# Four modulation units of layer 1 computed during layer 0's top-k rounds, the last two weight steps of three products taken together per token tile, and four row products moved to GpSimd

## Chip, cores, metric

The kernel runs on one core of a Trainium2 chip. The metric is the device time of one launch in microseconds, median of three runs. Everything is float32; products that need full precision are split into a high and a low half in the rounded format `float32r` and done as three matmuls.

## What is computed

A two-layer diffusion-style transformer block (512 image tokens, 256 context tokens, width 1024) followed by a second, causal block. Cut to what matters:

```python
for i in range(2):                                   # "layer 0" and "layer 1"
    mods  = silu(c)     @ ada_w[i] + ada_b[i]        # 6 x 1024 modulation values from a vector
    cmods = silu(c_ctx) @ ada_w[i] + ada_b[i]
    h  = rms_norm(x, n1) * (1 + sc1) + sh1           # same for the context rows
    p  = h @ w_in[i]                                 # five conv columns, window attention, global attention
    x  = x + g1 * (concat(ya, yb, yc, yd) @ w_out[i])            # "mix"
    h2 = rms_norm(x, n2) * (1 + sc2) + sh2
    aff = softmax(h2 @ router)                       # 16 experts
    gates, idx = top_k(aff.T, capacity)              # 64 image tokens, 32 context tokens per expert
    y  = (silu(xs @ w_gate) * (xs @ w_up)) @ w_down  # per expert, on the tokens picked
    x  = x + g2 * scatter_add(y * gates)
x = rms_norm(x, final_g)                             # then the second block:
x = x + concat(gated_deltanet(..), dilated_attention(..)) @ w_out_2      # on rms_norm(x, ln1_2)
x = x + (silu(conv(h @ w_gate_2)) * (h @ w_up_2)) @ w_down_2             # h = rms_norm(x, ln2_2)
out = rms_norm(x, ln_f_2)
```

Context rows are needed in layer 0 only. `ada_w[i]` is 1024 x 6144; a **modulation unit** `(l, u)` is the product with 512 of its columns, so there are 12 units a layer.

## The kernel before

It is written per engine: functions `sync`, `tensor`, `scalar`, `vector` and `gpsimd` each issue one engine's instructions in a fixed order, with semaphore waits that name what they need (`P[...]` from TensorE, `A[...]` ScalarE, `V[...]` VectorE, `G[...]` GpSimd). Tables shared by all five set the order of mixed work: `attention_plan` and `experts_plan`.

**Weights.** `weight_steps` lists every weight load, 1 MB each, in the order of use. SyncE issues them one after the other (L723). Each goes into a slot: three slots of `RING`, a fourth that is the context half of `X` (layer 1 and later), three of `WIDE`. `WIDE` shares its memory with `WHL`, which holds split weights; so a `WIDE` load waits until the last product with split weights (`ld["after"]`) is over. A load waits also until the step that last used its slot is over, and whatever stands behind it in SyncE's list waits too. The row stores of layer 0 (`xrows` L701: the tokens, to which the experts' results are added by scatter; `hrows` L704: the normalised tokens, from which later experts gather) stand in the same list, ahead of the load marked `rows`.

**Modulation units** (`ada`): two loads, for each 4 x 32-column matmuls into one bank (L772), ScalarE copies the row to `ROW4` (L1319), TensorE turns it (L764), VectorE adds the bias (L1826). Units 0 to 3 of layer 0 are done at the start. The other 8 of layer 0 and all 12 of layer 1 are spread over layer 0's attention, one for each pair of heads in `attention_plan`; a pair is scores (L901, L898), softmax on VectorE and ScalarE (L2078, L1445), two flips (L910, copied by L1458), values (L921, L926) and background work such as `spread` (L857).

**Mix**: `tokens` does a product of token tiles (6 in layer 0, 4 later) with a weight of 8 x 128 rows, half of the columns at a time, in four steps of 256 rows. A step does six matmuls on each tile in turn (L1090 to L1092). The results are read tile by tile after the last step of a half: VectorE scales (L2126) and GpSimd or VectorE adds to `X` (L2594, L2129); in the second half `behind` runs the norm as well, ScalarE squares (L1322), takes the root (L1326) and VectorE scales the tile (L1845). In this order VectorE takes tile t's sum, then tile t-1's mean square, then tile t-2's scaling, and after the last tile all that is left.

**Route**: TensorE turns the tiles (L782, L756), ScalarE and VectorE copy them (L1484, L2138), router product (L951), softmax, then eight rounds of top-8 on VectorE (L2171, L2173), a scan for the places (L2177, L2179), and `posT` on TensorE (L971), after which the experts' tokens are selected (L2207) and picked (L1037, L1040).

**Experts**: 12 loads each; per load 4 matmuls with the image tokens (L983), 4 with the context tokens in layer 0 (L989).

**Between the blocks**: for each of four tiles, `final_g` multiplies the tile (L2506, VectorE), ScalarE squares the tile and the product (L1322), roots, and VectorE scales the product (L2500); both norms are made from these. At its end the second block has two products in the form of `tokens`, `mix2` and `down2`, each followed by a norm through `behind`.

Of the kernel before, what the change touches and what calls it, by code (L numbers as in the profile page):

```python
# [8 lines left out]
ALU = mybir.AluOpType  # L9
# [6 lines left out]
LOOK = 2  # L16

# [79 lines left out]
def weight_steps(ada_w, w_in, w_out, w_gate, w_up, w_down, w_in2, w_out2, w_gate2, w_up2, w_down2):  # L97
# [29 lines left out]
    for l in range(2):  # L127
# [5 lines left out]
        if l == 0:  # L133
            ada(0, range(4, 12))
            ada(1, range(12))
        for half in (0, 512):
            add(w_out[l, :, half:half + 512], 8, 512, "k")
        for e in range(17):
# [7 lines left out]
            if e == 0:  # L146
                wide = len(loads) - 4
# [5 lines left out]
        for ld in loads[wide - 4:]:  # L153
            ld["expert"] = True
    for c0 in (0, 512, 1024):
        add(w_in2[:, c0:c0 + 512], 8, 512, "f")
# [18 lines left out]

    turn, slots, last, count = -1, (), {}, {}
    q, last_q, nq, wide, split = -1, {}, 0, None, None
    for ld in loads:
        turn, slots = (0 if ld["slots"] != slots and slots[:3] != ld["slots"][:3] else turn + 1), ld["slots"]
        k = slots[turn % len(slots)]  # L180
# [15 lines left out]
    for used in range(len(steps)):  # L196
# [4 lines left out]
        while done < len(steps) and done <= used + LOOK:  # L201
            if used < mix <= done:
                break
# [8 lines left out]
def attention_plan(l, need_ctx):  # L212
# [5 lines left out]
    units = [(0, u) for u in range(4, 12)] + [(1, u) for u in range(12)] if need_ctx else []  # L218
# [290 lines left out]
def program(nc, vecs, rows, frow, heads, consts, hconst, bias, x, ctxt, ada_w, w_in, w_out, router,  # L509
            w_gate, w_up, w_down, w_in2, w_out2, w_gate2, w_up2, w_down2, out):  # L510
    with ExitStack() as es:
# [103 lines left out]
        ONES = TM1[0:48, :]  # L615
# [40 lines left out]
        XG, HN2, JUNK = ar(0, 4, 1024), ar(4096, 4, 1024), [ar(8192, 1024), ar(9216, 1024)]  # L656
# [73 lines left out]
        def tensor(e):  # L730
# [351 lines left out]
            def tokens(ring, name, on, k, n, hi, lo_, nt=4):  # L1082
                st, h, lo = weights()
                for t in range(nt):
# [3 lines left out]
                    for i in range(2):  # L1088
                        j = n + i
                        e.matmul(o, hi(j)[:, z], h[:, i, :], start=j == 0, stop=False)  # L1090
                        e.matmul(o, hi(j)[:, z], lo[:, i, :], start=False, stop=False)  # L1091
                        ins = e.matmul(o, lo_(j)[:, z], h[:, i, :], start=False, stop=j == k - 1)  # L1092
                    names = [(*name, t)] if n == k - 2 else []
                    if t == nt - 1:
                        ins.then_inc(pe, P(("w", st["i"]), *names))
                    elif names:
                        ins.then_inc(pe, P(*names))
# [180 lines left out]
            for half in range(2):  # L1278
                for n in range(0, 8, 2):
                    tokens(every, ("mix2", half), V, 8, n, lambda j: YH2[j], lambda j: YL2[j])  # L1280
            turn_tiles(HN3, "2c", lambda j: ("x3T", j), lambda j: (V, ("x3T", j)))
            for part, r0, pairs in ffn_plan():
                columns([(V, ("gate", f)) for f, _ in pairs], "x3T")
                columns([(V, ("gu", f)) for f, _ in pairs])
                if pairs[-1][0] == FFN[part][1] // 128 - 1:
                    nf = (FFN[part][1] - r0) // 128
                    e.wait_ge(dve, V["gl", FFN[part][1] // 128 - 1])
                    for half in range(2):
                        for n in range(0, nf, 2):
                            tokens(every, ("down2", part, half), V, nf, n, lambda j: GH[:, j, :], lambda j: GL[:, j, :])  # L1290


        def scalar(e):
# [185 lines left out]
            def route(l, need_ctx):  # L1479
# [11 lines left out]
                e.activation(aff, aff, ACT.Exp).then_inc(act, A(("eaff", l)))  # L1491

# [284 lines left out]
            for half in range(2):  # L1777
                tokens(8)
            normalise(HN3, "2c", [(dve, V["mix2", 1, t]) for t in range(4)])
# [996 lines left out]
```

## Time and profile before

| | |
|---|---|
| median of 3 runs | 2863.82 us (2863.59 to 2863.98) |
| profiled execution, device time | 2861.94 us |
| its span, first to last instruction | 2860.1 us |
| TensorE matmuls busy | 2589.9 us, 91% |
| VectorE, ScalarE, GpSimd busy | 46%, 35%, 12% |
| mean granted TensorE clock | 0.963 |
| moved from and to DRAM | 567.72 MB, mean 198 GB/s |

Where the time lies, by the span's own clock: start and layer 0's first product to 200 us, layer 0 attention to 387, mix to 455, route to 508, experts to 1112, layer 1 attention to 1379, mix to 1425, route to 1470, experts to 1989, the turn to the second block to 2030, the second block to 2860. A busy share of 91% says that most of the span is TensorE's, but not in which stage something else ends last; this is read from the timelines of the stages. A row of a timeline gives start, duration, engine, line, the operation, and in brackets the idle time before it with the engine that ended it.

### The profile page before, as it was taken

To read this page: it belongs to the slowest core of one execution; us is meant where nothing else is said; L and a number is where in the kernel's file an instruction comes from. 1 tells how busy PE (TensorE), PEld (TensorE's weight loads), DVE (VectorE), ACT (ScalarE), POOL (GpSimd) and SP (SyncE) were. 2 spreads that over 40 slices of the span, in tenths; PEclk is the share of its full clock that TensorE was granted. 3 is DMA by queue.
4 is the path that set the end of the run, shared out by engine and by line. 5 is a ranking of instruction groups with operands and counts; after the bars stand their busy time and mean duration, and the time that the engine had idled before them with its cause. 6 is when DMAs were issued, how large, how long until landed. Compare 5 with 4: busy or idle time off the path is not lost.

```text
span 2860.1 us, 35448 instructions
## 1 busy us (share of the span) xinstructions
PE 2589.9 (91%) x13952; PEld 1523.0 (53%) x13952; DVE 1312.8 (46%) x2567; ACT 1004.2 (35%) x1857; POOL 348.5 (12%) x186
## 2 busy tenths in 40 slices
PE   6999996999999996987869999997899997999998
PEld 3875575322222222764733333332567786787886
DVE  2597545344444444676342333323654654443342
ACT  4226542343444444446322222221343333322222
POOL 0210020010011101210200000000114220222221
PEclk9999998999999998999979999999899898999999
DMA  7218732799999998210139999999120002223221
GB/s 249 74 45 281 250 103 103 267 320 367 366 362 366 361 371 270 85 60 1 64 143 386 386 386 386 386 386 349 31 89 30 16 12 79 95 89 98 94 81 52
DMA packets 303036, 567.72 MB, mean 198 GB/s; under 512 B 12624, under 2 KB 55760, under 8 KB 302744
## 3 DMA queue, kind: packets, MB, share of 16 engines
q1 hardware_dynamic: 294480, 545.33, 53.5%
q0 software_dynamic: 3616, 11.80, 1.8%
q10 hardware_dynamic: 4776, 8.33, 0.9%
q8 instruction: 112, 1.84, 0.3%
q14 instruction: 52, 0.43, 0.0%
HBM read 550.74 MB, written 14.68 MB: 198 GB/s over the span
## 4 chain that ended last, share of the span: by engine, by line
PE 42%; DMA 5%; DVE 4%; ACT 1%; issue 1%; POOL 0%; DVEq 0%; ACTq 0%; SPq 0%
PE PS L983 9%; PE PS L1079 4%; PE PS L1078 4%; PE PS L1077 4%; PE PS L1090 3%; PE PS L1092 3%; PE PS L1091 3%; PE PS L1037 2%; PE PS L1067 2%; DMA WIDE<-in_w_gate_dram 1%; PE PS L756 1%; DMA RING<-in_w_gate_dram 1%; PE PS L1194 1%; PE PS L1199 1%; PE PS L1122 1%
## 5 line engine op out<-in xcount | busy, mean ns | idle before, releaser
L2578 POOL TENSOR_TENSOR WHL<-RING,WHL 128x1024 fp32r<-128x1024 f32 x64 | 173.2, 2707 | 1594.5 <-ACT WHL L1310 1594.5
L983 PE MATMUL PS<-RING,RF 128*64 128x512 f32 x1448 | 350.3, 609 | 17.9 <-DMA RING<-in_w_gate_dram 6.2
L983 PE MATMUL PS<-WIDE,RF 128*64 128x512 f32 x1408 | 331.0, 600 | 8.8 <-DMA WIDE<-in_w_up_dram 3.2
L1310 ACT ACTIVATE WHL<-RING 128x1024 fp32r<-128x1024 f32 x129 | 134.5, 1047 | 231.7 <-PE PS L1092 145.1
L983 PEld LDWEIGHTS PS<-RING,RF 128*64 128x64 f32 x1448 | 92.3, 137 | 225.0 <-issue 199.6
L1077 PE MATMUL PS<-RR,WHL 128*128 128x512 f32 x512 | 205.2, 401 | 1.1 <-DVE RR L2329 1.1
L1079 PE MATMUL PS<-RR,WHL 128*128 128x512 f32 x512 | 205.3, 401 | 0.0
L1078 PE MATMUL PS<-RR,WHL 128*128 128x512 f32 x512 | 203.2, 397 | 0.0
L983 PEld LDWEIGHTS PS<-WIDE,RF 128*64 128x64 f32 x1408 | 92.7, 136 | 201.8 <-issue 181.6
L1559 ACT ACTIVATE RF<-PS,MODS,MSC 128x128 f32<-128x128 f32 x192 | 77.6, 438 | 292.6 <-PE PS L1037 155.1
L1813 DVE TENSOR_TENSOR WHL<-RING,WHL 128x1024 fp32r<-128x1024 f32 x65 | 79.6, 1225 | 185.9 <-ACT WHL L1310 185.9
L2263 DVE TENSOR_TENSOR RF<-PS,RF 64x512 f32<-64x512 f32 x64 | 43.6, 681 | 183.1 <-ACT RF L1543 183.1
L1092 PE MATMUL PS<-WHL,AS 128*128 128x512 f32 x288 | 115.5, 401 | 0.0
L2236 DVE TENSOR_TENSOR RF<-PS,RF 64x512 f32<-64x512 f32 x64 | 43.5, 680 | 150.7 <-ACT RF L1508 150.6
L1897 DVE SCALAR_TENSOR_TENSOR AR<-AR,VEC 128x497 f32<-128x497 f32 (+29 forms) x180 | 111.8, 697 | 0.0
L1077 PEld LDWEIGHTS PS<-RR,WHL 128*128 128x128 f32 x512 | 97.0, 189 | 26.5 <-issue 2.5
L1078 PEld LDWEIGHTS PS<-RR,WHL 128*128 128x128 f32 x512 | 96.9, 189 | 26.4 <-issue 1.7
L1079 PEld LDWEIGHTS PS<-RR,WHL 128*128 128x128 f32 x512 | 96.9, 189 | 22.3
L1090 PE MATMUL PS<-WHL,AS 128*128 128x512 f32 x248 | 100.3, 404 | 8.2 <-DVE AS L2559 4.3
L2236 DVE TENSOR_TENSOR AR<-PS,AR 64x512 f32<-64x512 f32 x64 | 43.6, 681 | 135.5 <-ACT AR L1508 135.5
L989 PE MATMUL PS<-RING,RF 128*32 128x512 f32 x776 | 99.9, 605 | 0.0
L1091 PE MATMUL PS<-WHL,AS 128*128 128x512 f32 x248 | 99.6, 402 | 0.0
(381 smaller groups left out, 4870.4 us busy)
## 6 DMA issues: line engine op xcount, KB each, us to landing
RING<-in_w_gate_dram SPq DMA_DIRECT2D x83, 1024.0 KB, 9.5
WIDE<-in_w_down_dram SPq DMA_DIRECT2D x74, 1024.0 KB, 9.3
RING<-in_w_up_dram SPq DMA_DIRECT2D x70, 1024.0 KB, 8.0
WIDE<-in_w_up_dram SPq DMA_DIRECT2D x57, 1024.0 KB, 11.9
RING<-in_w_down_dram SPq DMA_DIRECT2D x51, 1024.0 KB, 14.0
RING<-in_ada_w_dram SPq DMA_DIRECT2D x48, 1024.0 KB, 6.6
WIDE<-in_w_gate_dram SPq DMA_DIRECT2D x45, 1024.0 KB, 11.2
RING<-in_w_in_dram SPq DMA_DIRECT2D x30, 1024.0 KB, 5.3
```

The lines of the kernel that those rows point to most:

```text
L983: ins = e.matmul(a[r:r + 64, :], xs[:, j, 0:64], w[:, i, :], start=j < 2, stop=j > 5)
L989: ins = e.matmul(b[r:r + 32, :], xs[:, j, 64:96], w[:, i, :], start=j < 4, stop=j > 3)
L1077: e.matmul(o, h[:, j, :], HTH2[:, j, :], start=j == 0, stop=False)
L1078: e.matmul(o, h[:, j, :], HTL2[:, j, :], start=False, stop=False)
L1079: ins = e.matmul(o, lo[:, j, :], HTH2[:, j, :], start=False, stop=j == 7)
L1090: e.matmul(o, hi(j)[:, z], h[:, i, :], start=j == 0, stop=False)
L1091: e.matmul(o, hi(j)[:, z], lo[:, i, :], start=False, stop=False)
L1092: ins = e.matmul(o, lo_(j)[:, z], h[:, i, :], start=False, stop=j == k - 1)
L1310: e.activation(h, load_buffer(ld)[:, js, cs], ACT.Copy).then_inc(act, A(("hi", st["i"])))
L1897: e.scalar_tensor_tensor(y, UB[:, i, t0 + lo + d:t0 + hi + d], VEC[:, w:w + 1], y, ALU.mult, ALU.add).then_inc(dve, V(*([("conv", l, s)] i ...
L2236: e.tensor_tensor(dst, held("upA", l, ex, half, w)[0:64, :], dst, ALU.add).then_inc(dve, V(("upA", l, ex, half, w)))
L2578: e.tensor_tensor(lo, load_buffer(loads[st["load"]])[:, js, cs], h.bitcast(F32), ALU.subtract).then_inc(pool, G(("lo", st["i"])))
```

## The change

1. `GAP_UNITS`: units 8 to 11 of layer 1 leave `attention_plan` (20 units become 16) and are done in `route` of layer 0: TensorE after the affinities are turned and before `posT`, ScalarE after the exponential, VectorE after the places. Their 8 loads follow `w_out`'s in the list. The first three loads of expert 0 now go to `WIDE` and stand behind the first three of these 8; the next three go to `RING` behind all 8; the row stores stand behind those.
2. `tokens` with `steps=2`: the last two steps of the second half of `mix` (both layers), of `mix2` and of `down2` run together, twelve matmuls on a tile before the next tile.
3. The products with `final_g` move from VectorE to GpSimd; the squares write to separate places (`JUNK` has four parts, and `HN2`).
4. `ONES` moves, since `ROW4` shares memory with its old place.

```diff
         if l == 0:
             ada(0, range(4, 12))
-            ada(1, range(12))
+            ada(1, range(GAP_UNITS[0]))
         for half in (0, 512):
             add(w_out[l, :, half:half + 512], 8, 512, "k")
+        gap = len(loads)
+        if l == 0:
+            ada(1, GAP_UNITS)
...
+        if l == 0:
+            for n, ld in enumerate(loads[own:own + 3]):
+                ld["slot"] = 4 + n
+            loads[gap + 3:own + 3] = loads[own:own + 3] + loads[gap + 3:own]
...
-    units = [(0, u) for u in range(4, 12)] + [(1, u) for u in range(12)] if need_ctx else []
+    units = [(0, u) for u in range(4, 12)] + [(1, u) for u in range(GAP_UNITS[0])] if need_ctx else []
...
             def mix_out(l, need_ctx):
                 for half in range(2):
-                    for n in range(0, 8, 2):
+                    for n in range(0, 8 - 4 * half, 2):
...
+                tokens(every, ("mix", l, 1), V, 8, 4, lambda j: YHI[j], lambda j: YLO[j], 6 if need_ctx else 4, 2)
...
+                if need_ctx:
+                    for u in GAP_UNITS:
+                        for q in range(2):
+                            ada(every, 1, u, q)
+                        if u > GAP_UNITS[0]:
+                            ada(every, 1, u - 1, 3)
+                    ada(every, 1, GAP_UNITS[-1], 3)
...
-            def tokens(ring, name, on, k, n, hi, lo_, nt=4):
-                st, h, lo = weights()
+            def tokens(ring, name, on, k, n, hi, lo_, nt=4, steps=1):
+                held_steps = [weights() for _ in range(steps)]
                 for t in range(nt):
...
+                    for m, (st, h, lo) in enumerate(held_steps):
+                        for i in range(2):
+                            j = n + 2 * m + i
+                            e.matmul(o, hi(j)[:, z], h[:, i, :], start=j == 0, stop=False)
...
             for t in range(4):
                 e.wait_ge(dve, V["sent", 1, 7, t, 1])
-                square(JUNK[0], "2a", t, X, 0)
-                e.wait_ge(dve, V["xg", t])
-                square(JUNK[1], "2b", t, XG, 16)
+                square(HN2[:, t, :], "2a", t, X, 0)
+                e.wait_ge(pool, G["xg", t])
+                square(JUNK[t], "2b", t, XG, 16)
...
-                e.wait_ge(dve, V["sent", 1, 7, t, 1])
-                e.tensor_tensor(XG[:, t, :], X[:, t, :], FG, ALU.mult).then_inc(dve, V(("xg", t)))
...
+            e.wait_ge(rows_in, 16)
+            for t in range(4):
+                e.wait_ge(dve, V["sent", 1, 7, t, 1])
+                e.tensor_tensor(XG[:, t, :], X[:, t, :], FG, ALU.mult).then_inc(pool, G(("xg", t)))
```

In `mix2` the order on ScalarE and VectorE also changes: the split of the step after next (`WHL<-X`, 128x1024) stood before the norm of the tiles and now stands behind it.

What TensorE has from the router's logits to `posT` in layer 0. Before (L960 logits, L756 affinities turned, L971 `posT`, L1037 the first pick):

```order
L960 MATMUL PS<-SM,VECY 128x16 x6
L756 MATMUL PS<-CON,AR 16x128 x6
L971 MATMUL PS<-CON,AR 128x16 x6
L1037 MATMUL PS<-AR 128x128 x4
L1040 MATMUL PS<-AR 128x64 x2
```

And of the change (L787 is the product of a modulation unit, L779 its turn, L994 `posT`):

```order
L976 MATMUL PS<-SM,VECY 128x16 x6
L771 MATMUL PS<-CON,AR 16x128 x6
L787 MATMUL PS<-RING,S 32x512 x16
L779 MATMUL PS<-SM,TM 128x2 x4
L787 MATMUL PS<-RING,S 32x512 x8
L779 MATMUL PS<-SM,TM 128x2 x4
L787 MATMUL PS<-RING,S 32x512 x8
L779 MATMUL PS<-SM,TM 128x2 x8
L994 MATMUL PS<-CON,AR 128x16 x6
L1060 MATMUL PS<-AR 128x128 x4
L1063 MATMUL PS<-AR 128x64 x2
```

All 32 products and 16 turns of the four units stand between the affinities and `posT`, which must wait for the last of them.

SyncE's list from layer 0's attention to the first experts, before:

```order
L723 DMA RING<-in_ada_w_dram 128x4x512 x40
L723 DMA RING<-in_w_out_dram 128x4x512 x4
L723 DMA RING<-in_w_gate_dram 128x4x512 x2
L723 DMA RING<-in_w_up_dram 128x4x512
L701 DMA xrows<-X 128x1024 x6
L704 DMA hrows<-AR 128x1024 x6
L723 DMA RING<-in_w_up_dram 128x4x512
L723 DMA WIDE<-in_w_gate_dram 128x4x512 x2
L723 DMA WIDE<-in_w_up_dram 128x4x512
```

And of the change:

```order
L738 DMA RING<-in_ada_w_dram 128x4x512 x32
L738 DMA RING<-in_w_out_dram 128x4x512 x4
L738 DMA RING<-in_ada_w_dram 128x4x512 x3
L738 DMA WIDE<-in_w_gate_dram 128x4x512 x2
L738 DMA WIDE<-in_w_up_dram 128x4x512
L738 DMA RING<-in_ada_w_dram 128x4x512 x5
L738 DMA RING<-in_w_up_dram 128x4x512
L738 DMA RING<-in_w_gate_dram 128x4x512 x2
L716 DMA xrows<-X 128x1024 x6
L719 DMA hrows<-AR 128x1024 x6
L738 DMA WIDE<-in_w_up_dram 128x4x512 x2
```

Six expert loads instead of three stand ahead of the row stores, and the stores stand behind the last load of the units.

VectorE between the blocks, first tile, before (L2301 the last sums into `X`, L2506 the product with `final_g`):

```order
L2301 TENSOR_TENSOR X<-PS,X 128x512 x8
L2506 TENSOR_TENSOR AR<-X,VECY 128x1024
L1837 TENSOR_SCALAR SM<-SM 128x1
L2511 RECIPROCAL SM<-SM 128x1
L2514 TENSOR_SCALAR SM<-SM 128x1
L2516 TENSOR_SCALAR SM<-SM 128x1
L2506 TENSOR_TENSOR AR<-X,VECY 128x1024
```

And of the change, VectorE:

```order
L2336 TENSOR_TENSOR X<-PS,X 128x512 x8
L1869 TENSOR_SCALAR SM<-SM 128x1
L2545 RECIPROCAL SM<-SM 128x1
L2548 TENSOR_SCALAR SM<-SM 128x1
L2550 TENSOR_SCALAR SM<-SM 128x1
L1869 TENSOR_SCALAR SM<-SM 128x1
```

The products are gone from VectorE; on GpSimd four of them stand together, one split behind the last sums of layer 1.

## Rows read from the trace of the kernel before

**Rows 1.** Timeline of TensorE, one pair of layer 0's attention with a unit.

```profile
348.37 1.92 PE L772 MATMUL PS<-RING,S 128*32 128x512 f32 x16
...
352.81 0.87 PE L910 MATMUL PS<-CON,RF 128*128 128x128 f32 x6
353.52 0.95 PE L764 MATMUL PS<-SM,TM 128*128 128x2 f32 x8
354.58 0.88 PE L910 MATMUL PS<-CON,VECY 128*128 128x128 f32 x6
...
357.06 1.93 PE L772 MATMUL PS<-RING,S 128*32 128x512 f32 x16
```

**Rows 2.** Timeline of TensorE, pairs of layer 1's attention, without units.

```profile
1363.72 0.88 PE L910 MATMUL PS<-CON,VECY 128*128 128x128 f32 x6
1365.49 0.87 PE L910 MATMUL PS<-CON,RF 128*128 128x128 f32 x6 [0.90 <-ACT RF L1458]
...
1369.47 0.88 PE L910 MATMUL PS<-CON,RF 128*128 128x128 f32 x6
```

**Rows 3.** Timeline of TensorE, route of layer 0.

```profile
475.55 1.44 PE L756 MATMUL PS<-CON,AR 128*16 128x128 f32 x6 [1.86 <-DVE AR L2161]
492.33 0.58 PE L971 MATMUL PS<-CON,AR 16*128 16x16 f32 x6 [15.34 <-DVE AR L2179]
494.68 2.04 PE L1037 MATMUL PS<-AR 128*128 128x128 f32 x8 [1.77 <-DVE AR L2207]
...
500.32 1.11 PE L1037 MATMUL PS<-AR 128*128 128x128 f32 x8
```

**Rows 4.** Stretches: busy us of PE, PEld, DVE, ACT, POOL; clock; DMA share; GB/s.

```profile
484.00:488.00 4.00, 0.00 (x0) 0.00 (x0) 3.83 (x9) 0.00 (x0) 0.00 (x0) 0.50 0.00 0
```

**Rows 5.** The same view in layer 1's experts.

```profile
1500.00:1600.00 100.00, 96.22 (x461) 37.38 (x458) 30.31 (x57) 24.57 (x47) 0.00 (x0) 1.00 1.05 386
```

**Rows 6.** DMA issues by line: count, size each, median us to landing.

```profile
RING<-in_w_in_dram SPq DMA_DIRECT2D x30, 1024.0 KB, 5.3
```

**Rows 7.** Timeline of TensorE at the start: units that wait for loads.

```profile
26.75 1.93 PE L772 MATMUL PS<-RING,S 128*32 128x512 f32 x8 [1.05 <-DMA RING<-in_ada_w_dram]
28.62 1.87 PE L764 MATMUL PS<-SM,TM 128*128 128x2 f32 x8
```

**Rows 8.** Timeline of SyncE's queue, route of layer 0.

```profile
461.46 6.21 SPq L704 DMA_DIRECT2D hrows<-AR  x6
511.23 0.38 SPq L723 DMA_DIRECT2D RING<-in_w_up_dram  x1
```

**Rows 9.** Timeline: last matmul of layer 0's mix, VectorE's last scaling.

```profile
454.82 0.39 PE L1092 MATMUL PS<-WHL,RR 128*128 128x512 f32 x1
...
463.86 0.75 DVE L1845 TENSOR_SCALAR AR<-X,SM 128x1024 f32<-128x1024 f32 x1
```

**Rows 10.** Timeline: end of layer 1's mix (load released), VectorE's last scaling.

```profile
1424.79 0.92 SPq L723 DMA_DIRECT2D WIDE<-in_w_gate_dram  x2
...
1431.50 0.75 DVE L1845 TENSOR_SCALAR AR<-X,SM 128x1024 f32<-128x1024 f32 x1
```

**Rows 11.** Timeline of VectorE between the blocks.

```profile
2008.98 1.22 DVE L2506 TENSOR_TENSOR AR<-X,VECY 128x1024 f32<-128x1024 f32 x1
...
2027.50 0.75 DVE L2500 TENSOR_SCALAR AR<-AR,SM 128x1024 f32<-128x1024 f32 x1
```

**Rows 12.** Timeline: a VectorE product with two SBUF inputs beside one of GpSimd.

```profile
1992.53 2.43 POOL L2578 TENSOR_TENSOR WHL<-RING,WHL 128x1024 fp32r<-128x1024 f32 x1 [566.52 <-ACT WHL L1310]
...
1992.68 2.83 DVE L2291 TENSOR_TENSOR AR<-RF,AR 64x512 f32<-64x512 f32 x1
```

**Rows 13.** Timeline of VectorE: last scaling in `mix2`, last scaling of the output.

```profile
2470.11 0.75 DVE L1845 TENSOR_SCALAR AR<-X,SM 128x1024 f32<-128x1024 f32 x1
...
2855.78 1.29 DVE L1847 SCALAR_TENSOR_TENSOR AR<-X,SM,VECY 128x1024 f32<-128x1024 f32 x1
```

**Rows 14.** Waits of TensorE in layer 0's experts, 640 to 1140 us: us, times, longest.

```profile
...
PE PS L1033 <- DMA AR<-hrows,IDX: 0.4, 1, 0.4
```

More of the change, by code:

```diff
@@ L16 @@
 LOOK = 2
+GAP_UNITS = range(8, 12)
 FFN = ((0, 1536), (1536, 2816))
@@ L146, in weight_steps @@
             if e == 0:
-                wide = len(loads) - 4
+                own = len(loads) - 8
+        wide = own + 4 if l else own + 6
         if l == 1:
@@ L152, in weight_steps @@
             ld["slots"] = (4, 5, 6, 0, 1, 2) + (3,) * l
-        for ld in loads[wide - 4:]:
+        for ld in loads[own:]:
             ld["expert"] = True
+        if l == 0:
+            for n, ld in enumerate(loads[own:own + 3]):
+                ld["slot"] = 4 + n
+            loads[gap + 3:own + 3] = loads[own:own + 3] + loads[gap + 3:own]
     for c0 in (0, 512, 1024):
@@ L174, in weight_steps @@
         st["behind"] = True
+    for n, ld in enumerate(loads):
+        for st in ld["steps"]:
+            st["load"] = n
     turn, slots, last, count = -1, (), {}, {}
@@ L178, in weight_steps @@
     for ld in loads:
-        turn, slots = (0 if ld["slots"] != slots and slots[:3] != ld["slots"][:3] else turn + 1), ld["slots"]
-        k = slots[turn % len(slots)]
+        if "slot" in ld:
+            k = ld["slot"]
+        else:
+            turn, slots = (0 if ld["slots"] != slots and slots[:3] != ld["slots"][:3] else turn + 1), ld["slots"]
+            k = slots[turn % len(slots)]
         count[k] = count.get(k, 0) + 1
@@ L201, in weight_steps @@
         while done < len(steps) and done <= used + LOOK:
-            if used < mix <= done:
+            if used < start <= done or used < mix <= done:
                 break
@@ L655, in program @@
         HTH2, HTL2 = rr(0, 8, 512), rr(4096, 8, 512)
[L656 removed]
+        XG, HN2, JUNK = ar(0, 4, 1024), ar(4096, 4, 1024), [ar(8192 + 1024 * t, 1024) for t in range(4)]
         KTOK, VTOK = ar(0, 4, 4, 128), ar(2048, 4, 4, 128)
@@ L1087, in tokens @@
                     o, z = held(*name, t), slice(128 * t, 128 * t + 128)
[L1088 to L1097, printed above, removed]
+                    for m, (st, h, lo) in enumerate(held_steps):
+                        for i in range(2):
+                            j = n + 2 * m + i
+                            e.matmul(o, hi(j)[:, z], h[:, i, :], start=j == 0, stop=False)
+                            e.matmul(o, hi(j)[:, z], lo[:, i, :], start=False, stop=False)
+                            ins = e.matmul(o, lo_(j)[:, z], h[:, i, :], start=False, stop=j == k - 1)
+                        names = [(*name, t)] if n + 2 * m == k - 2 else []
+                        if t == nt - 1:
+                            ins.then_inc(pe, P(("w", st["i"]), *names))
+                        elif names:
+                            ins.then_inc(pe, P(*names))
             def attend2(ring, i):
@@ L1278, in tensor @@
             for half in range(2):
-                for n in range(0, 8, 2):
+                for n in range(0, 8 - 4 * half, 2):
                     tokens(every, ("mix2", half), V, 8, n, lambda j: YH2[j], lambda j: YL2[j])
+            tokens(every, ("mix2", 1), V, 8, 4, lambda j: YH2[j], lambda j: YL2[j], 4, 2)
             turn_tiles(HN3, "2c", lambda j: ("x3T", j), lambda j: (V, ("x3T", j)))
@@ L1288, in tensor @@
                     for half in range(2):
-                        for n in range(0, nf, 2):
+                        last = 4 * (part == half == 1)
+                        for n in range(0, nf - last, 2):
                             tokens(every, ("down2", part, half), V, nf, n, lambda j: GH[:, j, :], lambda j: GL[:, j, :])
+                        if last:
+                            tokens(every, ("down2", part, half), V, nf, nf - 4, lambda j: GH[:, j, :], lambda j: GL[:, j, :], 4, 2)
         def scalar(e):
@@ L1491, in route @@
                 e.activation(aff, aff, ACT.Exp).then_inc(act, A(("eaff", l)))
+                for u in GAP_UNITS if need_ctx else ():
+                    for q in range(3):
+                        ada(1, u, q)
             def experts(l, need_ctx):
@@ L1776, in scalar @@
             between()
-            for half in range(2):
-                tokens(8)
+            tokens(8)
+            tokens(6)
             normalise(HN3, "2c", [(dve, V["mix2", 1, t]) for t in range(4)])
+            tokens(2)
             e.dma_start(VECY, frow[1:2, :].to_broadcast([128, D])).then_inc(rows_in, 16)
@@ L2302, in experts, with tokens @@
                                         ).then_inc(dve, V(("sent", l, g, t, half)))
-            def tokens(name, k, residual=False, key=None, gain=None):
-                for n in range(0, k, 2):
+            def tokens(name, k, residual=False, key=None, gain=None, later=0):
+                for n in range(0, k - 2 * later, 2):
                     weights()
@@ L2315, in tokens @@
                             behind(HN3, key, t, 3, gain)
+                for _ in range(later):
+                    weights()
             def convolve(o, name, taps, vcol, *finish):
@@ L2541, in vector @@
             for half in range(2):
-                tokens(("mix2", half), 8, True, "2c")
+                tokens(("mix2", half), 8, True, "2c", None, half)
             split2(HTH2, HTL2, "x3T", V_LN2)
```

8 lines of the change are left out of this document (6 added, 2 removed).

## The prediction

> **What bounds the kernel now.** I read the page first, then the stretches by stage, then the timelines of each engine where the change touches. TensorE is the engine that ends last in layer 0's attention: between two units it has no idle time, and a pair of heads with a unit takes 357.06 - 348.37 = 8.69 us [rows 1]. In route it waits: from the affinities (475.55 + 1.44 = 476.99) to `posT` at 492.33 it has nothing, VectorE works alone, and DMA moves nothing [rows 3, 4]. Layer 0's experts are TensorE's again, with no wait for a weight load [rows 14]. Layer 1's experts are DMA's at 386 GB/s [rows 5], so 1 MB (1.049 MB) takes 2.72 us, and they shift as a whole with their start. So whatever shortens attention, the two mixes, the turn between the blocks or the tail comes through whole; what grows in route is paid whole.
>
> **1. Units out of attention.** Removed from four pairs: 32 matmuls on 1 MB loads, 1.92 us a unit by its row, 1.86 us to the start of what follows since rows overlap by some 0.06, and the turn L764, 0.95 us [rows 1]. The turn stands between the two flips, whose starts are 354.58 - 352.81 = 1.77 us apart. In layer 1, without units, they are 1365.49 - 1363.72 = 1.77 us apart as well, 0.90 of it a wait for ScalarE [rows 2]. The turn is hidden in that wait, and taking it away exposes the wait: 0 us saved. A whole pair of layer 1 takes 1369.47 - 1363.72 = 5.75 us [rows 2]; with the background's spread (some 1.08 us of TensorE a pair in layer 0) that would be 6.83 against 8.69, again 1.86. Four times 1.86 is 7.4; the last turn falls in a pair of context queries with shorter waits, where I give 0.4 more. **7.8 us.** Bounds: 6.0 if a new wait of some 0.5 us shows in three of the four pairs, 4 x (1.86 + 0.95) = 11.2 if nothing takes the turn's place.
>
> **2. Joint last steps.** The matmuls are the same; only the order is. Tiles of the second half are ready 2.82 us apart (twelve matmuls of 0.235 us) instead of 1.41, and the last at the same time, so all but the last tiles are through the norm before the product ends. I laid out `behind` with the rows' durations.
> - Layer 0's mix ends at 454.82 + 0.39 = 455.21 and the last scaling at 463.86 + 0.75 = 464.61 [rows 9], 9.4 us later. With tiles early, behind the last one stand its product and sum on VectorE (1.4), the square (1.25), the scalings of tiles 3 and 4 in between, mean square, root, reciprocal and scaling: 5.3 us. The copies for the router start on VectorE behind it, so **4.1 to 4.7**, I take 4.6 (TensorE's 32 turns no longer follow the last scaling). This is not a gain by itself: see 3.
> - Layer 1's mix ends at 1424.79, the last scaling at 1431.50 + 0.75 = 1432.25 [rows 10]: 7.5 us, with joint steps 5.2. **2.3 us** (bounds 1.5 and 3.5).
> - `mix2`: the last scaling ends at 2470.11 + 0.75 = 2470.86 [rows 13]. Its order on VectorE (two scalings behind the last sum) leaves 0.4 us, and the split moved behind the norm (ScalarE 1.04, VectorE 1.23 us) now stands ahead of the first copies, part of it in their wait for TensorE. **0** (-0.6 to 0.5).
> - `down2`: the last scaling ends at 2855.78 + 1.29 = 2857.07 [rows 13]; laid out anew it ends at 2855.4. **1.7 us** (1.0 to 2.5).
>
> **3. Units in route.** The first 3 of 8 loads are in place early; SyncE's queue then waits with the fourth until the first is used. A load on its own lands in 5.3 us [rows 6], queued ones follow 2.72 apart [rows 5]. So with the start of the units as zero and full clock (a load used in 0.96 us, half of 1.93): the fourth is issued at 1.0, lands at 6.2, the eighth 4 x 2.72 later at 17.1; then 1.0 of product, two turns and `posT`: 20.4 us. The units start 4.6 us earlier than 476.99, at 472.4, which gives `posT`'s end at 492.8; before it ended at 492.91 [rows 3]. So at full clock route's joint gain is eaten to within 0.1 us. The top-k rounds would have been over some 4 us earlier.
>
> The clock is what I know least. In the gap it was at its 1.2 GHz level (0.50) after idle TensorE [rows 4], and there a load takes 1.93 and a turn 1.87 us [rows 7]. All of it at that level: the chain is TensorE's in part, `posT` ends at about 496.7, 3.8 us later than before. Dense work first brings the clock back: the picks began at 2.04 us and were at 1.11 some 5 us on [rows 3]. The three loads in place are 5.8 us of dense work at the low level, so I take the clock as high from the third load on: `posT` at 493.7, 0.8 us late; and the picks no longer start low, which returns 1.4 us. **+0.6 us** for joint step and units together (-2.5 to 2.5).
>
> The Trainium skill (TensorE: Matmul & The Clock Gate, Part 1: The HAM clock gate) says that an idle array runs at half its clock and that sustained work restores it; these rows agree. By that rule alone, a TensorE that mostly waits for loads could be held at the low level, which is the 3.8 us case.
>
> **4. Expert loads and stores.** Six loads are in place when the experts begin instead of three, but TensorE did not wait for loads there, so nothing is gained. The stores, issued by 467.7 before [rows 8], now go out behind the units' last use, at about 490 to 496, 12 x 0.5 MB or 16.3 us at 386 GB/s, done near 512. The seventh expert load is due on TensorE at about 525 and needs 5.3 us from 511. **0 us** (-4 to 0).
>
> **5. Products on GpSimd.** Before, the first product starts at 2008.98, behind the last sum, and the last scaling ends at 2028.25 [rows 11]: product, square of the product (1.25), root, reciprocals in a ring of 4.4 us a tile. On GpSimd a product takes about 2.4 us [rows 12] and starts with its tile's sum at 2002.9, so all four are over by 2012.8. The ring is then ScalarE's: two squares (2.3) and two roots, 2.7 us a tile; the last scaling ends at 2022.1. **6.1 us.** Bounds 4.5 and 7. VectorE can be stopped by GpSimd: a product with two inputs in SBUF took 2.83 us beside GpSimd's 2.43 [rows 12]. The sums that run beside these read PSUM and one tile, and the first scaling comes at 2013.6, behind them; if it meets the last product, it costs up to 2.4 once.
>
> The Trainium skill (SBUF — State Buffer, Who interferes with whom) has the shared ports as an exclusive lock for two SBUF inputs or a two-port mode, and free otherwise: it names the same ops, so its sum would be mine.
>
> **Sum:** 7.8 + 0.6 + 2.3 + 0 + 1.7 + 0 + 6.1 = 18.5 us from the profiled execution's 2861.94: 2843.4. The median of the runs shown is 1.88 above that execution, so 2845.3.
>
> **Rivals.**
> - *The turn's time comes back in attention* (11.2 instead of 7.8), and the joint steps give their upper bounds: about 5 us more, 2840. Against it: equal distances of the flips in both layers. 0.17.
> - *The units overrun the top-k rounds*: low clock, or loads that land further apart than 2.72. `posT` 4 to 6 us late, the turn between blocks at its lower bound: 2850. For it: the gap is short for 8 loads, and no row shows TensorE's clock at such work in this place. 0.18.
> - *The change of `final_g` brings nothing*, since ScalarE's own ring is slower than laid out or GpSimd holds VectorE: about 6 us less, 2851. 0.06.
> - *Slower than before*: the row stores, now in one stretch with the experts' loads, starve TensorE. They would have to end so late that the seventh load comes more than 18.5 + 5.7 = 24 us after it is due at 525, that is, 12 stores would take over 50 us instead of 16.3. Gathers wait for them too, but only from 558 on. 0.03.
>
> **How the numbers follow.** My forecast (2841.5 to 2848.5) has 0.56. The likeliest time is 2845.3. The range takes in the rivals at 2840 and 2851: 2838.5 to 2852. A measurement of this kernel can tell about 0.2%, 5.7 us, from no change. Faster by more than that needs under 2858.1: all cases but the starved one and the case that several terms fall short together: 0.95. Within 0.2%: 0.03. Slower: 0.02.
>
> **What would show it.** Right: pairs of layer 0 without units at 6.8 us, a wait of 0.9 between flips; no idle stretch of 15 us in route, `posT` within 2 us of where it stood against the mix's end, its releaser a unit's turn; between the blocks 2.7 us a tile; no TensorE wait for `WIDE` or `RING` in layer 0's experts. Wrong: pairs below 6.3 us; `posT` released by VectorE's places; TensorE's clock at 0.5 through the gap; a wait for DMA near 525.

## The result, and the profile after

Over ten runs of each, the changed kernel takes 2854.47 us (median; 2849.27 to 2855.94), the kernel before 2863.03: a ratio of 0.9968 (95% interval 0.9958 to 0.9977), 8.6 us faster. I had forecast 18.5 us less and 2845.3. The profiled execution took 2851.78 us, 2.7 below the median, and its span is 2849.9, 10.2 less than before's. One execution of `held_experts` below took 3779.85 us at a mean clock of 0.649, in a slow state, and is left out of its median and ratio. I read the two traces stage by stage, each from one event to the next (from start to start of the instructions named).

| stretch | before | after | difference | forecast |
|---|---|---|---|---|
| start to the end of layer 0's attention | 387.17 | 386.39 | -0.8 | -7.8 |
| layer 0's mix, to its last matmul | 67.65 | 67.66 | 0.0 | 0 |
| to `posT` | 37.51 | 44.18 | +6.7 | +0.8 |
| to the first expert matmul | 15.90 | 16.05 | +0.2 | -1.4 |
| layer 0's experts, to layer 1's first turn | 625.30 | 624.85 | -0.5 | 0 |
| to layer 1's last scaling in mix | 297.97 | 295.67 | -2.3 | -2.3 |
| to layer 1's first expert matmul | 38.51 | 37.83 | -0.7 | 0 |
| layer 1's experts, to the last sum | 538.36 | 538.57 | +0.2 | 0 |
| to the last scaling between the blocks | 19.13 | 10.45 | -8.7 | -6.1 |
| to the last scaling of `mix2` | 442.61 | 440.34 | -2.3 | 0 |
| to the last scaling of the output | 385.67 | 383.62 | -2.1 | -1.7 |

0.5 of the 0.8 us in the first line was there at 218 us, before anything that the edit touches. These are single executions: in `before` and the three kernels below that leave attention as it was, the first line is 387.15 to 389.40. The first, third and fourth lines miss by more than the whole; others give part of it back. Timeline of TensorE in the changed kernel, where the last unit has just been used (L925 flips, L936 and L941 values, L872 `spread`, L916 and L913 scores); the pair answers to [rows 1]:

```profile
336.61 0.87 PE L925 MATMUL PS<-CON,RF 128*128 128x128 f32 x6
...
338.77 0.39 PE L941 MATMUL PS<-CON,SM 128*64 128x128 f32 x4
342.98 1.36 PE L872 MATMUL PS<-TM,CON 128*128 128x128 f32 x8 [3.82 <-DVE RF L2131]
344.27 2.08 PE L916 MATMUL PS<-RF 64*128 64x512 f32 x4
346.13 1.06 PE L913 MATMUL PS<-RF 64*128 64x256 f32 x4
...
348.92 0.88 PE L925 MATMUL PS<-CON,RF 128*128 128x128 f32 x6 [0.90 <-ACT RF L1486]
...
352.18 1.16 PE L872 MATMUL PS<-TM,CON 128*128 128x128 f32 x8 [0.70 <-DVE RF L2131]
...
356.54 0.87 PE L925 MATMUL PS<-CON,VECY 128*128 128x128 f32 x6 [0.90 <-ACT RF L1486]
```

The 0.90 us between the flips is there, as forecast. What is new stands ahead of `spread`: 0.70 us in each pair, and 3.82 in the first. That pair lasts 348.92 - 336.61 = 12.31 us, the next 7.62, where I had 6.83 for each. 3.82 is the wait, and of the remaining 1.66 us 1.61 are the scores and `spread` at the low clock after it (2.08 for 1.13, 1.06 for 0.60, 1.36 for 1.16): 6.83 + 3.82 + 1.66 = 12.31.

Why VectorE is late there: its timeline, with GpSimd's beside it (L1845 and L2612 are the two halves of a split of `w_out`, L2086 the gate's products, L2131 the sum for which `spread` waits).

```profile
333.98 1.22 DVE L1845 TENSOR_TENSOR WHL<-RING,WHL 128x1024 fp32r<-128x1024 f32 x1 [0.66 <-ACT WHL L1338]
335.12 2.91 DVE L2086 TENSOR_TENSOR AR<-AR 128x256 f32<-128x256 f32 x2
...
342.63 0.29 DVE L2131 TENSOR_TENSOR RF<-PS,SM 128x128 f32<-128x128 f32 x1 [1.14 <-ACT SM L1492]
```

```profile
334.97 2.44 POOL L2612 TENSOR_TENSOR WHL<-RING,WHL 128x1024 fp32r<-128x1024 f32 x1 [141.65 <-ACT WHL L1338]
```

Splits run two steps ahead of the product, and a step of a unit counts as one. With four units fewer, the first two splits of `w_out` come four pairs earlier. There they meet the gate: two products of 128x256 last 2.91 us. In before the same two, and GpSimd's half of the split, stood apart:

```profile
333.83 0.75 DVE L2054 TENSOR_TENSOR AR<-AR 128x256 f32<-128x256 f32 x2
```

```profile
368.46 2.45 POOL L2578 TENSOR_TENSOR WHL<-RING,WHL 128x1024 fp32r<-128x1024 f32 x1 [174.66 <-ACT WHL L1310]
```

Route, TensorE (L787 a load's product, L779 a turn, L994 `posT`); it answers to [rows 3]:

```profile
469.62 1.02 PE L771 MATMUL PS<-CON,AR 128*16 128x128 f32 x6 [1.85 <-DVE AR L2193]
470.56 4.22 PE L787 MATMUL PS<-RING,S 128*32 128x512 f32 x24
477.83 1.94 PE L787 MATMUL PS<-RING,S 128*32 128x512 f32 x8 [3.06 <-DMA RING<-in_ada_w_dram]
...
491.89 1.93 PE L787 MATMUL PS<-RING,S 128*32 128x512 f32 x8 [2.63 <-DMA RING<-in_ada_w_dram]
493.76 1.87 PE L779 MATMUL PS<-SM,TM 128*128 128x2 f32 x8
496.46 1.83 PE L779 MATMUL PS<-SM,TM 128*128 128x2 f32 x8 [0.84 <-ACT TM L1347]
498.23 0.61 PE L994 MATMUL PS<-CON,AR 16*128 16x16 f32 x6
```

The stretches of route (us of PE, PEld, DVE, ACT, POOL; clock; DMA share; GB/s):

```profile
474.00:476.00 2.00, 0.78 (x8) 0.00 (x0) 1.90 (x5) 0.59 (x1) 0.00 (x0) 1.00 0.88 312
476.00:478.00 2.00, 0.17 (x4) 0.17 (x8) 1.93 (x4) 0.00 (x0) 0.00 (x0) 0.73 0.98 337
478.00:480.00 2.00, 2.00 (x10) 0.34 (x6) 1.90 (x6) 0.00 (x0) 0.00 (x0) 0.50 1.03 367
...
498.00:500.00 2.00, 0.83 (x8) 0.71 (x7) 1.29 (x9) 0.00 (x0) 0.00 (x0) 0.50 0.99 316
```

The fourth load is used 7.3 us after the start (forecast 6.2), the clock does come back with the first three loads (1.00 from 474), falls again in the wait for the fourth and stays at 0.50 to the end, in this execution. `posT` starts 27.7 us behind the first product; the top-k rounds need 15.3.

Between the blocks, ScalarE and GpSimd, which answer to [rows 11]:

```profile
2013.14 1.04 ACT L1350 ACTIVATE AR<-AR 128x1024 f32<-128x1024 f32 x1
...
2015.40 1.04 ACT L1350 ACTIVATE AR<-AR 128x1024 f32<-128x1024 f32 x1
```

```profile
2005.92 9.29 POOL L2659 TENSOR_TENSOR AR<-X,VECY 128x1024 f32<-128x1024 f32 x4 [8.07 <-DVE X L2336]
```

A tile takes 2.26 us where I had 2.7 (4.37 before), and GpSimd makes a product in 9.29 / 4 = 2.3 us beside VectorE's sums, which take 0.69 us as before.

### The profile page after: what moved, and what is told of

Same layout as the page of the kernel before. It is cut to its first block, busy times and chain, and to the rows that moved or that the text cites. A ratio compares the mean times of both kernels' runs of the same rounds, so it can differ in the third digit from the quotient of the medians.

```text
span 2849.9 us, 35453 instructions
## 1 busy us (share of the span) xinstructions
PE 2597.6 (91%) x13952; PEld 1522.7 (53%) x13952; DVE 1310.9 (46%) x2563; ACT 1004.3 (35%) x1857; POOL 355.8 (12%) x190
## 4 chain that ended last, share of the span: by engine, by line
PE 42%; DMA 5%; DVE 3%; ACT 1%; issue 1%; DVEq 0%; ACTq 0%; SPq 0%
PE PS L1006 9%; PE PS L1101 4%; PE PS L1100 4%; PE PS L1102 4%; PE PS L1114 3%; PE PS L1115 3%; PE PS L1116 3%; PE PS L1060 2%; PE PS L1090 2%; DMA WIDE<-in_w_gate_dram 1%; PE PS L771 1%; DMA RING<-in_w_gate_dram 1%; PE PS L1218 1%; PE PS L1223 1%; PE PS L1132 1%
## 5 line engine op out<-in xcount | busy, mean ns | idle before, releaser
L2612 POOL TENSOR_TENSOR WHL<-RING,WHL 128x1024 fp32r<-128x1024 f32 x64 | 173.1, 2705 | 1563.6 <-ACT WHL L1338 1563.6
L1006 PE MATMUL PS<-RING,RF 128*64 128x512 f32 x1440 | 341.7, 604 | 12.1 <-DMA RING<-in_w_gate_dram 5.5
L1006 PE MATMUL PS<-WIDE,RF 128*64 128x512 f32 x1416 | 339.3, 606 | 14.1 <-ACT RF L1590 4.5
L1845 DVE TENSOR_TENSOR WHL<-RING,WHL 128x1024 fp32r<-128x1024 f32 x65 | 79.6, 1225 | 186.9 <-ACT WHL L1338 186.9
L1012 PE MATMUL PS<-WIDE,RF 128*32 128x512 f32 x768 | 99.4, 607 | 0.0
## 6 DMA issues: line engine op xcount, KB each, us to landing
WIDE<-in_w_gate_dram SPq DMA_DIRECT2D x75, 1024.0 KB, 10.2
```

The lines of the kernel that those rows point to most:

```text
L1006: ins = e.matmul(a[r:r + 64, :], xs[:, j, 0:64], w[:, i, :], start=j < 2, stop=j > 5)
L1012: ins = e.matmul(b[r:r + 32, :], xs[:, j, 64:96], w[:, i, :], start=j < 4, stop=j > 3)
L2612: e.tensor_tensor(lo, load_buffer(loads[st["load"]])[:, js, cs], h.bitcast(F32), ALU.subtract).then_inc(pool, G(("lo", st["i"])))
```

## The experiments

Twelve kernels, in three sets of four, each set on one chip with the kernel before (2860.96, 2860.47 and 2861.02 us). Ratios are to that, with 95% intervals. The changed kernel was not in these sets, so a comparison with it goes by its own ratio, 0.9958 to 0.9977.

**One part at a time.** Four kernels take the diff's parts apart: the units' move (parts 1 and 4 of the change) in `gap_only`, the joint steps with `mix2`'s order (part 2) in `joint_only`, the products (part 3) in `finalg_only`, and the last two together in `joint_finalg`.

> The kernel before with the four modulation units moved into route, nothing else of the change. Theory from the trace of the changed kernel: attention gives back 0.2 us only, and the chain of loads, products and turns lasts 27.6 us from the first unit to posT where the top-k rounds last 15.3, so route is 12.3 us longer: 11 to 12 us slower than before, about 2874.5 us; the granted clock at 0.50 from the affinities to the picks. My prediction's terms give for this part alone 7.8 us less in attention and 5.3 more in route: 2.5 us faster, 2860.5. If the move of the units is not what ate the gain, this run is within 3 us of before.

Measured: 2875.99 us, 1.0048 (1.0031 to 1.0065), 15 us slower.

```profile
475.96 1.44 PE L771 MATMUL PS<-CON,AR 128*16 128x128 f32 x6 [1.86 <-DVE AR L2186]
...
504.68 0.60 PE L993 MATMUL PS<-CON,AR 16*128 16x16 f32 x6
```

From the affinities to `posT` 28.7 us, against 16.8 before: 11.9 us longer, and attention ends at 387.44, not earlier at all. This execution is 13.9 us longer than before's; the picks take another 0.9. The rest differs stage by stage where the edit touches nothing, with both signs: layer 1's attention and mix +4.4 (295.2 us to mix's last matmul, 290.8 before; the clock of 1140 to 1180 us is 0.78 here and 1.00 in before's), to the last scaling of `mix2` -8.1, the last product +4.2.

> The kernel before with joint last steps in the four products, nothing else. Theory from the trace of the changed kernel: 5.2 us less at layer 0's mix (last product to affinities), 2.5 at layer 1's, 0.4 at mix2, 2.0 at down2: 10.1 us faster, about 2853. My prediction's terms: 4.6 + 2.3 + 0 + 1.7 = 8.6 us, about 2854.4. Rival: in layer 0 the early tiles only help because the units take the time; then the gain is 5 us.

Measured: 2854.05 us, 0.9977 (0.9966 to 0.9988), 6.9 us faster. By the trace the last scaling is 4.4 us earlier in layer 0 and 2.5 in layer 1, and the turns behind it bring another 0.8 in layer 0 and 0.7 in layer 1; 0.95 goes back in the picks (`posT` to experts 16.85 us against 15.90). 10 us in the stages that the edit touches; the rest of the span was 2 us longer.

> The kernel before with the four products with final_g on GpSimd, nothing else. Theory from the trace of the changed kernel: last scaling between the blocks 8.7 us earlier against the last sum, about 2854.3. My prediction's term: 6.1 us, 2856.9. Rival: part of the 8.7 us belongs to the other edits (the place of the squares' results, the clock); then under 6 us.

Measured: 2852.01 us, 0.9965 (0.9952 to 0.9978), 9.0 us faster. Last sum to last scaling: 10.37 us, against 19.13.

> The changed kernel with the four units back in layer 0's attention, that is joint last steps and products on GpSimd together. Theory: the parts add up, 10.1 + 8.7 = 18.8 us faster than before, about 2844, and so 10 us faster than the whole change: the move of the units is a loss of some 10 us. Rival (my prediction's terms): moving the units is a gain of 7.8 - 4.0 = 3.8 us, and this kernel is slower than the whole change, 2858 or more.

Measured: 2842.68 us, 0.9936 (0.9923 to 0.9948), 18.3 us faster than before and thus some 10 us faster than the whole change; the two intervals don't touch. The move of the units is the loss.

**Attention.** `late_split` keeps the units in route and puts the split back where it stood (`out_0` is `w_out`'s first step):

```diff
+    late = ahead[out_0 - 2] + ahead[out_0 - 1]
+    ahead[out_0 - 2] = ahead[out_0 - 1] = []
+    ahead.insert(out_0, late)
...
+        if n == 19 and need_ctx:
+            plan.append(("split",))
```

> The changed kernel, with the split of w_out's first two steps (two ScalarE copies, a VectorE and a GpSimd difference) moved from the last unit in layer 0's attention to the place where it stood before, four pairs later. Theory: in the changed kernel that split falls on the gate's products on VectorE (2.91 us there, 0.75 before), the sums for the next flip come late, TensorE stands 3.8 us and then runs some 3 us at the 0.50 clock; so this kernel is 4 to 4.7 us faster than the changed one, and its pair in question lasts some 7.6 us like its neighbours, with a wait of 0.7 left. Rival: the pair is late because the unit's matmuls were the cover of a chain of ScalarE and VectorE that is there anyway; then at most 1 us.

Measured: 2848.33 us, 0.9954 (0.9937 to 0.9970), 12.1 us faster than before, where the change is 8.6; the intervals overlap. VectorE's gate and TensorE's wait in this kernel:

```profile
336.08 0.75 DVE L2097 TENSOR_TENSOR AR<-AR 128x256 f32<-128x256 f32 x2
```

```profile
339.44 0.88 PE L932 MATMUL PS<-CON,RF 128*128 128x128 f32 x6
...
343.04 1.16 PE L879 MATMUL PS<-TM,CON 128*128 128x128 f32 x8 [1.04 <-DVE RF L2142]
...
347.40 0.88 PE L932 MATMUL PS<-CON,RF 128*128 128x128 f32 x6 [0.90 <-ACT RF L1495]
```

The pair takes 7.96 us for 12.31, the clock does not fall: 4.35 us, as expected. It is the pair that prices the split, not the run's time: ahead of this pair the execution stood 2.8 us behind the changed kernel's (339.44 against 336.61), a difference older than the edit's place, so that attention ends only 1.1 us earlier. The run moves ScalarE's copies, VectorE's difference and GpSimd's together; how much of the wait is each one's isn't shown.

Route, which this edit leaves alone, is 4.7 us shorter here than in the changed kernel:

```profile
470.98 3.82 PE L794 MATMUL PS<-RING,S 128*32 128x512 f32 x24
478.35 1.07 PE L794 MATMUL PS<-RING,S 128*32 128x512 f32 x8 [3.55 <-DMA RING<-in_ada_w_dram]
...
487.42 3.33 PE L794 MATMUL PS<-RING,S 128*32 128x512 f32 x16
...
493.52 0.56 PE L1001 MATMUL PS<-CON,AR 16*128 16x16 f32 x6
```

`posT` comes 22.5 us behind the first product, where the changed kernel has 27.7: the eighth load is used without a wait, and the last turns take 1.05 us, at the high clock. The same list of loads and products gives other times from one execution to the next; this has to be kept in mind for the route experiments below.

`late_bank7` adds this, on TensorE alone:

```diff
-  spread(small, l, 2, ...)
+  spread(ada_bank if last_unit in done_units else small, l, 2, ...)
```

> The kernel with the later split, and in addition the spread behind the last unit writes to the bank that the units no longer need, where it wrote to the one bank of the values. Theory: the 0.70 us wait for VectorE ahead of each spread is a wait for that bank; without it another 0.7 us in each of 4 pairs: 2 to 3 us faster than the kernel with the later split alone, 6.5 to 7.5 faster than the changed one, which is then the 7.4 of my prediction. Rival: the scores behind it then wait for ScalarE instead, and nothing is gained.

Measured: 2846.45 us, 0.9950 (0.9934 to 0.9967), 1.9 us better than `late_split` by the medians, well within the intervals.

```profile
337.79 0.88 PE L933 MATMUL PS<-CON,RF 128*128 128x128 f32 x6
...
340.27 1.16 PE L879 MATMUL PS<-TM,CON 128*128 128x128 f32 x8
...
344.62 0.88 PE L933 MATMUL PS<-CON,RF 128*128 128x128 f32 x6 [0.90 <-ACT RF L1496]
```

The wait ahead of `spread` is gone, and the pair lasts 6.83 us, the number of my prediction. Attention ends at 380.12, 7.1 us earlier than before. Route keeps a delay: 26.7 us from the affinities to `posT`, 25.9 from the first product.

**Route.** First with two units, alone and with the two edits above, then with three:

```diff
-GAP_UNITS = range(8, 12)
+GAP_UNITS = range(10, 12)
```

> The changed kernel with two units in route and the other two back in attention (4 loads in route, 3 of them in place). Theory: the fourth load lands 5.3 us after the first use, the chain of TensorE ends near 484 us, before the last places of VectorE; posT follows VectorE as before, the route is 11.5 to 12 us shorter than the changed one's and attention 1 to 2 us longer, where the split falls elsewhere: about 2844, 10 us faster. Rival (the clock alone matters, not the number of loads): half of it, 5 us.

Measured: 2842.26 us, 0.9940 (0.9920 to 0.9961), 18.2 us faster than before.

```profile
479.90 1.07 PE L787 MATMUL PS<-RING,S 128*32 128x512 f32 x8 [3.91 <-DMA RING<-in_ada_w_dram]
...
487.63 0.64 PE L994 MATMUL PS<-CON,AR 16*128 16x16 f32 x6 [2.35 <-DVE MODS L1858]
```

`posT` waits for VectorE again, 16.8 us behind the affinities. The split now costs 2.23 us.

> Two units in route, the later split and the spread in the units' bank. Theory: route stays as with two units alone (posT behind VectorE's places), and attention loses the 2.2 us wait at the split and 0.7 us in each of the pairs without a unit: 3 to 4.5 us faster than two units alone, about 2838.5, 22 us faster than before. Rival: the waits move to ScalarE's flips and 1 us at most is gained.

Measured: 2840.47 us, 0.9934 (0.9921 to 0.9948): level with `joint_finalg`, and with two units alone within the intervals. The profiled execution (2847.6 us) is 7 us above the median, with the clock at 0.50 at the start of mix and low stretches in both attentions. Where the edits touch, they do what they should: the pair behind the last unit lasts 6.84 us, in `two_units` 9.13. How much that adds to the time isn't settled.

> The same with three units in route (6 loads). Theory: a third unit saves 1.8 us in attention, but its loads land 2.8 us apart, so TensorE's chain ends 4 to 6 us behind the last places: 2 to 4 us slower than with two units. Rival: the chain still ends with the places, and three units are 1.8 us faster than two.

Measured: 2843.33 us, 0.9941 (0.9926 to 0.9956). From the affinities to `posT` 20.6 us, 4.1 longer than with two, as expected, against 1.9 us that a unit saves in attention. The times don't tell it from two units.

The change again with its four units, and idle TensorE filled (`warm`, and with fewer fillers `warm_less`):

```diff
+  if 2 * (u - GAP_UNITS[0]) + q > 2:
+      fill = bank(every, ("fill", u, q))
+      for _ in range(3 if (u, q) == (GAP_UNITS[1], 1) else 2):
+          e.matmul(fill, IDN, CON[:, 0:512], start=True, stop=True)
```

> The changed kernel with idle TensorE filled: ahead of each of the units' last five loads two or three matmuls of 128x128 by 128x512 float32 on the identity, whose result nobody reads. Theory: with the array kept busy the clock stays at 1.00, a load takes 0.96 instead of 1.93 us and a turn 0.95 instead of 1.87; what is left is the spacing of the loads: posT 5 to 7 us earlier than in the changed kernel, about 2848.5. Rival: the loads set the chain (they land up to 8 us after their issue, beside the experts' loads), and the clock is high but posT gains under 2 us.

Measured: 2850.65 us, 0.9956 (0.9938 to 0.9973). The clock is high and no load is waited for:

```profile
482.00:486.00 4.00, 4.00 (x15) 1.30 (x15) 3.79 (x10) 0.60 (x1) 0.00 (x0) 1.00 1.03 377
```

First product to `posT`: 24.4 us, 3.3 less than the change, but 1.9 more than `late_split` took without any filler; the fillers, 0.95 us each, fill more than the loads leave. By the times, `warm` and the change can't be told apart.

```diff
-      for _ in range(3 if (u, q) == (GAP_UNITS[1], 1) else 2):
+      for _ in range(3 if (u, q) == (GAP_UNITS[1], 1) else 1):
```

> The changed kernel with fewer filler matmuls: three ahead of the units' fourth load and one ahead of each later load (7 instead of 11). Theory: in the run with 11 the clock was at 1.00 and no unit waited for its load, so the fillers themselves were what TensorE had too much of; with 7 the chain from the first product to posT is 20.5 to 22.5 us, against 27.7 in the changed kernel and 24.4 with 11 fillers, which is what my prediction has for full clock (20.4). Rival: with less filling the clock falls to 0.50 and the chain is 25 us or longer.

Measured: 2853.68 us, 0.9970 (0.9959 to 0.9981). In its trace the chain is 22.5 us, with TensorE's waits for loads at 0.35 to 0.61: here the loads set the pace, at full clock. It is also the length that `late_split` had without fillers, so no gain of theirs is shown. The time shows none either: 2 us went to layer 0's experts (626.7) and 4 to layer 1's attention (295.2), which no edit touches.

```diff
+            loads[own + 3]["held"] = loads[own - 1]["steps"][-1]["i"]
...
+                if "held" in ld:
+                    e.wait_ge(pe, P["w", ld["held"]])
```

> The changed kernel, with the first of the experts' loads behind the units (and so all loads and stores behind it) held until TensorE has used the units' eighth load. Theory: the eighth load took 8.4 us from issue to landing, where the fourth took 5.3, because the experts' load issued 2.2 us later shares the DMA with it; held, it lands some 2.8 us sooner, and posT with it (28.6 us from the affinities to posT become about 26). Rival: the chain is TensorE's at the low clock, and posT moves by under 1 us; the experts then wait for their loads.

Measured: 2855.0 us, 0.9981 (0.9969 to 0.9993). From the affinities to `posT` 25.75 us against 28.61: 2.9 us, as expected, with the clock at 0.50 still.

```profile
488.03 3.64 PE L790 MATMUL PS<-RING,S 128*32 128x512 f32 x16
```

The seventh and eighth load now follow without a wait. But so they do in `late_split`, which holds nothing back: there the stage takes 23.87 us, and 26.65 in `late_bank7`. So the 2.9 us lie within what the stage varies by from one execution to the next, and aren't shown to come from the hold. The profiled execution has 2851.49 us, the changed kernel's 2851.78, and the interval begins at 0.9969, above the change's ratio: no gain in the time.

## Why the prediction was wrong

- **Term 1, units out of attention: 7.8 forecast, 0.8 measured, 0.5 of it not the edit's.** The step that failed is that a pair without its unit, "with the background's spread", "would be 6.83". The size is right (6.83 in `late_bank7`), but taking the matmuls out had two effects that I put at nothing. One is the wait of `spread` for the only bank of the values, 0.70 us a pair: I had looked only at the turn's cover, between the flips, and layer 1's attention, from whose pairs I took the form, has two such banks. The other is that the table of splits counts steps: I had left the splits of `w_out` where they stood, and eight steps less moved them onto the gate, which cost 3.1 us of wait (3.82 less 0.70) and 1.66 of clock. 3.1 + 1.7 + 4 x 0.7 = 7.6 us, all of the gain. Shown by the pairs of `late_split` and `late_bank7`, and by attention's end in `late_bank7`, 7.1 us before that of before.
- **Term 3, route: a gain of 0.6 us forecast, a loss of 6.8 measured**, the rival of the overrun, which I gave 0.18. Three steps failed. "I take the clock as high from the third load on": it came back, and was lost in the next wait of 3.06 us, for the rest of the chain. (The 1.4 us that the picks were to win from a high clock stayed out for the same reason.) "queued ones follow 2.72 apart": from the fourth landing to the eighth it took 14.1 us in the changed kernel, not 4 x 2.72 = 10.9; in `late_split` it took 10.9. Whether the experts' load beside the eighth makes the difference isn't shown. And a load takes 5.3 us from an issue that comes 2.0 us after the first product, not 1.0. That four units overrun is shown by all seven traces that have them: the chain took 27.7 us in the changed kernel, 27.4, 25.9 and 22.5 in others that leave it as it is, 24.4 with the loads held back, 24.4 and 22.5 with fillers, and never my 20.4. Even at 22.5 (`late_split`) the stretch from mix's last matmul to the experts is 2.5 us longer than in before and 7.0 longer than in `joint_only`: four units don't fit into this gap, two do. Whether the clock or the loads make it 22.5 or 27.7 stays open.
- **Term 2, joint steps.** Layer 0: 4.4 to the last scaling (4.6 forecast) and 0.8 in the turns, which I had not counted. Layer 1: 2.5 (2.3), and 0.7 in the turns. By `joint_only`, `mix2` gives 0.4 (0 forecast) and `down2` 2.0 (1.7).
- **Term 5, between the blocks: 6.1 forecast, 8.7 measured**, beyond my upper bound of 7. The mechanism was right, the size was not: a tile takes 2.26 us, two squares of 1.04 that follow without a gap and the roots' 0.18, where I had 2.7; and the load of the roots' table (1.28 us) and the first product are over before the last sum.
- **Term 4, loads and stores: 0, right.** TensorE waits for no `WIDE` or `RING` load in layer 0's experts.

The two misses have one sign. Attention is 7.0 us above its forecast and route 7.4; the turn between the blocks gives 2.6 back, and `mix2`, layer 1's route, the experts and the last product 3.5: together the 8.3 us by which the profiled execution's span missed. The rivals held each miss alone; my range had no case with both, and ended 2.5 us too low.

## What to carry to other kernels

Before work is taken off the busy engine, list what waits under it: every bank, buffer or sum that the next instruction needs, not only the neighbour. Where a lookahead counts steps, taking steps out moves everything that hangs on the count; compare its place on the other engines before and after. A gap can be filled with what is in place when it begins; each further load costs its landing. Here even that brought nothing measurable: the best kernel with units in the gap is at 0.9934, the one without any at 0.9936. The parts of such a change are best timed one by one, since here 18 us of gain hid 10 us of loss; and before a few us between two single traces are put down to an edit, look at what the same stage takes in other kernels that leave it alone.

## What the runs showed of the hardware

The clock does not answer one wait always alike. Twice near the end of the last product TensorE waits 2.17 us for VectorE. In the kernel before the first of these waits drops the clock, the second doesn't (stretches as above):

```profile
2611.00:2613.00 2.00, 2.00 (x6) 1.55 (x5) 0.00 (x0) 0.00 (x0) 1.35 (x1) 0.50 0.03 8
...
2794.00:2796.00 2.00, 2.00 (x10) 1.64 (x9) 0.00 (x0) 0.00 (x0) 1.83 (x1) 1.00 0.03 8
```

So it is in `gap_only` and `finalg_only`. In `joint_only`, `joint_finalg` and the changed kernel it is the other way round; here `joint_only`:

```profile
2604.00:2606.00 2.00, 2.00 (x9) 1.63 (x10) 0.00 (x0) 0.01 (x1) 1.92 (x1) 1.00 0.11 39
...
2786.00:2788.00 2.00, 2.00 (x7) 1.54 (x7) 0.00 (x0) 0.00 (x0) 2.00 (x1) 0.60 0.07 23
```

Which one it is goes with the joint steps, in all fourteen traces: the first wait in the three kernels without them, the second in the eleven with them. A fall costs some 1.5 us (323.07 against 321.52 us from `mix2`'s last scaling to the second wait). Each trace has one, so the table above is not changed by it. Why one wait drops the clock and the other doesn't was not settled.

Stages that no edit touches differ between single executions, and the clock goes with it. From layer 1's first turn to its mix's last matmul the fourteen traces have 290.6 to 295.6 us, with the clock at 0.50 for 17 us of it in before (290.8) and 34 in `warm_less` (295.2). The stage that ends with `mix2`'s last scaling is 442.61 us in before, 440.34 in the changed kernel, 437.12 in `warm`, 434.54 in `gap_only`, whose edits end long ahead of it. Of the 2.3 us in its line above, 0.4 stands in `joint_only` as well and is the edit's; the other 1.9 gather at several stretches of low clock. One is at the stage's first products, which run at 0.50 for 3.6 us in before and 2.0 in the changed kernel. So a stage table of two single executions holds terms of 2 us and more that belong to no edit, and this may be why runs of one kernel spread over 7 us.

VectorE's work with two SBUF inputs was slowed beside GpSimd's product (2.91 us for two products of 0.75), GpSimd's was not (2.44 us, 2.45 apart from it); VectorE's sums from PSUM beside GpSimd's four products took their usual 0.69. The Trainium skill (SBUF — State Buffer, Who interferes with whom) tells the same two cases apart, VectorE with two inputs in SBUF and with at most one, and these rows agree.
